# Attention as an 18-unit pipeline in which each engine works on another unit, in a two-layer hybrid transformer step

## The reference

```python
def sink_softmax(logits, sink):
    s = jnp.broadcast_to(sink[None, :, :, None, None], logits.shape[:-1] + (1,))
    p = jax.nn.softmax(jnp.concatenate([s, logits], -1), axis=-1)
    return p[..., 1:]
...
q = axial_rope(q, row, col); k_att = axial_rope(k_att, row, col)     # latent tokens only
...
# latent block i of 128 queries: all 256 cached keys and the blocks i-1, i, i+1 of latent keys
s_c = jnp.einsum('bqkgd,bskd->bkgqs', qblk, ck) * scale
s_w = jnp.where(ok, jnp.einsum('bqkgd,bskd->bkgqs', qblk, kw) * scale, NEG_INF)
p = sink_softmax(jnp.concatenate([s_c, s_w], -1), sink)
out = einsum(p[..., :P], cv) + einsum(p[..., P:], vw)
```

## Time and profile before

| | |
|---|---|
| time, median of 3 runs | 3071.33 us (3064.5 to 3072.36) |
| the profiled execution | time 3057.68 us, span 3055.9 us |
| TensorE | 2703.0 us busy, 88% of the span |
| VectorE | 1314.2 us busy, 43% |
| ScalarE | 1057.0 us busy, 35% |
| GpSimd | 189.6 us busy, 6% |
| mean granted TensorE clock | 0.94 of full speed |

### The profile page before, as it was taken

One profiled execution on the slowest core, in us unless ns is written; L12 is line 12 of the kernel. 1 busy time (PEld: TensorE's weight loads), 2 busy tenths in 40 slices (PEclk: granted clock), 3 DMA queues, 4 the chain that ended last, 5 costly groups with the idle time before them and its releaser, 6 DMA issues.

```text
span 3055.9 us, 72861 instructions
## 1 busy us (share of the span) xinstructions
PE 2703.0 (88%) x32894; PEld 2345.9 (77%) x32894; DVE 1314.2 (43%) x2266; ACT 1057.0 (35%) x1809; POOL 189.6 (6%) x155
## 2 busy tenths in 40 slices
PE   5998699997879999997977899987689999999996
PEld 3985577786679996447955677876589999999995
DVE  2346344443342220004454444533356555555665
ACT  3225334432332120013234434422344444444442
POOL 0001111110000000000000111101010000000010
PEclk8998799997989999998989899988799999999998
DMA  6212033210112221111200131000165555555571
GB/s 243 77 62 113 1 114 113 76 42 2 59 49 76 76 76 62 62 55 59 76 30 1 58 114 59 4 3 4 56 236 209 199 190 207 207 207 186 201 251 74
DMA packets 82717, 304.87 MB, mean 100 GB/s; under 512 B 9376, under 2 KB 9504, under 8 KB 82272
## 3 DMA queue, kind: packets, MB, share of 16 engines
q1 hardware_dynamic: 71072, 257.93, 23.5%
q0 software_dynamic: 11328, 42.21, 3.7%
HBM read 273.10 MB, written 27.00 MB: 98 GB/s over the span
## 4 chain that ended last, share of the span: by engine, by line
PE 84%; DVE 6%; issue 4%; ACT 4%; POOLq 1%; DMA 1%; DVEq 0%; POOL 0%; SPq 0%; PEldq 0%; ACTq 0%
PE ps L401 16%; PE ps L403 16%; PE ps L402 16%; PE ps L1178 6%; PE ps L965 3%; PE ps L978 3%; PE ps L958 3%; PE ps L842 2%; PE ps L641 2%; PE ps L724 1%; PE ps L414 1%; PE ps L781 1%; PE ps L766 1%; PE ps L870 1%; POOLq L2360 1%
## 5 line engine op out<-in xcount | busy, mean ns | idle before, releaser
L1784 DVE TENSOR_TENSOR ring_lo<-ring,w_ffn 128x1024 fp32r<-128x1024 f32 x308 | 374.1, 1224 | 217.2 <-ACT w_ffn L1371 211.3
L401 PE MATMUL ps<-hg_hi,w_ffn 128*128 128x256 f32 x1408 | 401.5, 285 | 0.9 <-DVE hg_lo L2224 0.9
L402 PE MATMUL ps<-hg_lo,w_ffn 128*128 128x256 f32 x1408 | 397.2, 282 | 0.0
L403 PE MATMUL ps<-hg_hi,ring_lo 128*128 128x256 f32 x1408 | 396.7, 282 | 0.0
L1371 ACT ACTIVATE w_ffn<-ring 128x1024 fp32r<-128x1024 f32 x308 | 322.3, 1056 | 198.1 <-PE ps L403 197.3
L401 PEld LDWEIGHTS ps<-hg_hi,w_ffn 128*128 128x128 f32 x1408 | 266.5, 189 | 2.5 <-DVE hg_lo L2224 1.1
L402 PEld LDWEIGHTS ps<-hg_lo,w_ffn 128*128 128x128 f32 x1408 | 265.6, 189 | 1.2
L403 PEld LDWEIGHTS ps<-hg_hi,ring_lo 128*128 128x128 f32 x1408 | 266.2, 189 | 0.0
L401 PE MATMUL ps<-hT_hi,w_proj 128*128 128x320 f32 x672 | 210.9, 314 | 10.0 <-DVE hT_lo L1790 10.0
L401 PE MATMUL ps<-hT_ffn_hi,w_ffn 128*128 128x320 f32 x704 | 214.3, 304 | 5.1 <-DVE hT_lo L1790 5.1
L402 PE MATMUL ps<-hT_lo,w_ffn 128*128 128x320 f32 x704 | 218.6, 310 | 0.0
(11 more groups left out here) (314 smaller groups left out, 5273.2 us busy)
## 6 DMA issues: line engine op xcount, KB each, us to landing
ring<-in_blocks SPq DMA_DIRECT2D x484, 512.0 KB, 3.5
h_rows<-arena POOLq DMA_DIRECT2D x16, 512.0 KB, 10.1
arena<-h_rows POOLq DMA_DIRECT2D x7, 1024.0 KB, 10.2
y_rows<-arena POOLq DMA_DIRECT2D x7, 1024.0 KB, 6.6
x<-in_x_all SPq DMA_DIRECT2D x1, 2560.0 KB, 13.1
h_plain<-arena POOLq DMA_DIRECT2D x1, 2560.0 KB, 11.5
out_y_all<-x POOLq DMA_DIRECT2D x5, 512.0 KB, 2.9
w<-in_low POOLq DMA_DIRECT2D x2, 768.0 KB, 4.9
```

The lines of the kernel that those rows point to most:

```text
L401: nc.tensor.matmul(dst, w_hi, m_hi, start=start, stop=False)
L402: nc.tensor.matmul(dst, w_hi, m_lo, start=False, stop=False)
L403: return nc.tensor.matmul(dst, w_lo, m_hi, start=False, stop=stop)
L1784: V.tensor_tensor(ring_lo[:, n % RING, :], ring[:, n % RING, :], high[:, n % high.shape[1], :], ALU.subtract).then_inc(*E.sig("w_lo"))
```

## The change

There are 18 units instead of 20: the four context units become two, of four heads each. In step t each engine now works on another unit: TensorE does chunk 0 of turning t-3, scores(t), chunk 1 of t-3, the values of t-4, and chunk 2 of t-3. VectorE does the division of t-2, the maxima of t, and the copy out of t-4. ScalarE does the exponentials of t-1 with the copies of the chunks of t-3 between and behind them. A unit's maxima are one instruction instead of two. The copies of the turned cache move from VectorE to ScalarE, after the first exponentials. Of the five rotary parts two come at steps 0 and 1, the others at steps 2, 5 and 9, in PSUM banks 2 and 5 that 512-key units leave free, and the product with the sine is written back to PSUM instead of to a buffer in SBUF. On GpSimd the cosine products are spread likewise around the stores and the clearing transfers.

```diff
+        N_CTXU = 2
+        N_ATT = N_CTXU + 16
+        ROPE_BANK = (2, 5, 2, 5, 5)
+        ROPE_AT = {2: 2, 5: 3, 9: 4}
+        ROPE_BEFORE = {2: 2, 4: 3, 7: 4, 11: 5}
...
             def scores(l, t):
...
                 if t >= 2:
-                    pe.wait_ge(sem["at_exp"], 2 * (n - 1))
-                if t == 4:
-                    pe.wait_ge(sem["rope_ev"], 5 * (l + 1))
+                    pe.wait_ge(sem["at_exp"], n - 1)
+                if t == N_CTXU:
+                    pe.wait_ge(sem["kc_ev"], l + 1)
+                if t in ROPE_BEFORE:
+                    pe.wait_ge(sem["rope_ev"], 5 * l + ROPE_BEFORE[t])
...
             def att_phase(l):
 
+                for t in range(N_CTXU):
+                    scores(l, t)
+                    rope_turn(l, t)
                 pe.wait_ge(sem["misc_in"], 16 * 4 * (l + 1))
...
-                rope_turn(l, 0)
-                rope_turn(l, 1)
-                for t in range(N_PAIRS + 3):
-                    if t < N_PAIRS:
+                for t in range(2, N_ATT + 4):
+                    if 3 <= t < N_ATT + 3:
+                        turn_probs(l, t - 3, 0)
+                    if t < N_ATT:
                         scores(l, t)
-                    if 1 <= t <= 3:
-                        rope_turn(l, t + 1)
-                    if 2 <= t < N_PAIRS + 2:
-                        turn_probs(l, t - 2, 0)
-                        turn_probs(l, t - 2, 1)
-                    if 3 <= t:
-                        attend(l, t - 3)
-                    if 2 <= t < N_PAIRS + 2:
-                        turn_probs(l, t - 2, 2)
+                    if t in ROPE_AT:
+                        rope_turn(l, ROPE_AT[t])
+                    if 3 <= t < N_ATT + 3:
+                        turn_probs(l, t - 3, 1)
+                    if t >= 4:
+                        attend(l, t - 4)
+                    if 3 <= t < N_ATT + 3:
+                        turn_probs(l, t - 3, 2)
...
             def att_phase(l):
-                act.wait_ge(sem["rope_ev"], 5 * l + 2)
...
+                for t in range(N_ATT + 3):
+                    u = t - 1
+                    if 0 <= u < N_ATT:
+                        act.wait_ge(sem["at_max"], l * N_ATT + u + 1)
+                        if u >= 3:
+                            act.wait_ge(sem["at_tr"], chunk_no(l, u - 2))
+                        A(stat(u, 3), stat(u, 1), ACT.Exp).then_inc(*E.sig("act_step"))
+                        for h in range(len(heads_of(u)) - 1):
+                            probs(l, u, h)
+                    probs_ev(l, t - 3, 0)
+                    if 0 <= u < N_ATT:
+                        probs(l, u, len(heads_of(u)) - 1)
+                    probs_ev(l, t - 3, 1)
+                    probs_ev(l, t - 3, 2)
+                    if t == 1:
+                        act.wait_ge(sem["kc_tr"], l + 1)
+                        A(kcT[:, :], ps[:, 6, 0:PAST], ACT.Copy).then_inc(*E.sig("act_step"))
+                        A(kctok[:, :], ps[:, 6, PAST:PAST + P], ACT.Copy).then_inc(*E.sig("act_step"))
+                        A(vtok[:, :, :].rearrange("p i c -> p (i c)"), pair640(3), ACT.Copy).then_inc(*E.sig("kc_ev"))
...
             def rope(l, c):
...
-                V.tensor_tensor(tmp, ps[:, (1, 4)[c % 2], :], C("sin"), ALU.mult).then_inc(*E.sig("dve_step"))
+                V.tensor_tensor(turned, turned, C("sin"), ALU.mult).then_inc(*E.sig("dve_step"))
                 dve.wait_ge(sem["rope_cos"], 5 * l + c + 1)
                 dve.wait_ge(*E.own_last())
-                V.tensor_tensor(dst, dst, tmp, ALU.add).then_inc(*E.sig("rope_ev"))
+                V.tensor_tensor(dst, dst, turned, ALU.add).then_inc(*E.sig("rope_ev"))
...
             def att_phase(l):
...
+                for t in range(N_ATT + 4):
+                    if 2 <= t < N_ATT + 2:
+                        divide(l, t - 2)
+                    if t < N_ATT:
+                        dve.wait_ge(sem["at_s"], l * N_ATT + t + 1)
+                        V.tensor_reduce(by_tile(stat(t, 4)) if t < N_CTXU else stat(t, 4), scores_of(t), AX.X, ALU.max).then_inc(*E.sig("dve_step"))
...
+                    if t < 2:
+                        rope(l, t)
+                    if t in ROPE_AT:
+                        rope(l, ROPE_AT[t])
                     if t >= 4:
...
+                        out_ev(l, t - 4)
```

More of the change, by code:

```diff
@@ L431, in with_flag, with heads_of, query_block, query_tiles @@
                 body()
-        N_PAIRS = 4 * NT
-        def pair_of(t):
-            return (t, -1) if t < 4 else ((t - 4) // 4, (t - 4) % 4)
+        N_CTXU = 2
[3 more added lines that the diff above has]
+        ROPE_BEFORE = {2: 2, 4: 3, 7: 4, 11: 5}
+        def heads_of(t):
+            if t < N_CTXU:
+                return [(2 * t + c, g) for c in range(2) for g in range(2)]
+            return [((t - N_CTXU) // 4, g) for g in range(2)]
+        def query_block(t):
+            return -1 if t < N_CTXU else (t - N_CTXU) % 4
+        def query_tiles(t):
+            c = heads_of(t)
+            return slice(c[0][0], c[-1][0] + 1)
         def own_blocks(blkq):
@@ L741, in scores @@
                 put(0, a0, kcT[rows64(0), :])
-                put(1, a1 + PAST, kT[rows64(1), two[0]])
-                put(0, a0 + PAST, kT[rows64(0), two[0]])
+                put(1, a1 + PAST, kT[rows64(1), two])
+                put(0, a0 + PAST, kT[rows64(0), two])
                 edge = own[0] if blkq > 0 else own[1]
@@ L769, in attend @@
             def attend(l, t):
-                c, blkq = pair_of(t)
-                n = l * N_PAIRS + t
+                first = l * N_ATT
+                heads, blkq = heads_of(t), query_block(t)
                 nk = n_keys(blkq)
@@ L1879, in rope, with divide @@
                 dve.wait_ge(sem["rope_cos"], 5 * l + c + 1)
                 dve.wait_ge(*E.own_last())
-                V.tensor_tensor(dst, dst, tmp, ALU.add).then_inc(*E.sig("rope_ev"))
+                V.tensor_tensor(dst, dst, turned, ALU.add).then_inc(*E.sig("rope_ev"))
+            def divide(l, t):
+                n, nk = len(heads_of(t)), n_keys(query_block(t))
+                dve.wait_ge(sem["at_exp"], l * N_ATT + t + 1)
+                V.tensor_tensor(stat(t, 4), stat(t, 2), stat(t, 3), ALU.add).then_inc(*E.sig("dve_step"))
+                dve.wait_ge(*E.own_last())
+                V.reciprocal(stat(t, 2), stat(t, 4)).then_inc(*E.sig("dve_step"))
+                dve.wait_ge(*E.own_last())
+                if t < N_CTXU:
+                    pr = prob[:, t % 3, 0:n * nk].rearrange("p (h k) -> p h k", h=n)
+                    V.tensor_tensor(pr, pr, stat(t, 2).unsqueeze(2).broadcast_to([P, n, nk]), ALU.mult).then_inc(*E.sig("at_p"))
+                    return
+                for h in range(n):
+                    pr = prob[:, t % 3, h * nk:(h + 1) * nk]
+                    V.tensor_scalar(pr, pr, attst[:, t % 4, 2, h:h + 1], None, ALU.mult).then_inc(*E.sig("at_p" if h == n - 1 else "dve_step"))
@@ L2450, in _ @@
                 next_phase()
-                for c in range(5):
-                    dst = kT[:, CTX:T] if c == 0 else qT[:, c - 1, CTX:T]
-                    pool.wait_ge(sem["rope_mm"], 5 * l + c + 1)
-                    nc.gpsimd.tensor_tensor(dst, dst, C("cos"), ALU.mult).then_inc(sem["rope_cos"], 1)
+                rope_cos(l, 0)
+                rope_cos(l, 1)
                 pool.wait_ge(sem["kc_ev"], l + 1)
```

172 lines of the change are left out of this document (76 added, 96 removed).

## The result

| | before | after |
|---|---|---|
| median | 3069.8 us (3064.5 to 3072.4, 4 runs) | 3013.4 us (3011.1 to 3017.8, 4 runs) |
| profiled execution | 3057.7 us | 3015.1 us |
| TensorE busy | 2703.0 us | 2693.3 us |

The ratio is 0.982, with a 95% interval of 0.9802 to 0.9839: 1.8% faster, where 1.1% had been forecast.

The account below looks back on a forecast made before the run. A VectorE-ScalarE loop was taken as the attention's bound, TensorE next. Start, middle and end gave 97.0 and 92.8 us against 112.5 and 111.5, 34.2 less: 3023.5 from the profile, scaled to 3037 on the median; range 3022 to 3054.

Parts of the forecast that it names:

- The bound: Middle part of attention: a VectorE-ScalarE loop bounds a unit at 5.03 us before; TensorE is the bound after.
- the step: Latent units in the middle part: 18.5 us for four, 4.62 us a unit, at full clock.
- the start: From the attention phase's start to the first latent scores: 6.8 us against 20.9, 14.1 less.
- the last one of the sum: Whole program: the ratio of 3023.5 to the profiled 3057.7 us, applied to the median 3071.3, gives 3037.
- the price of the clock in layer 0: Middle part, layer 0: four steps with TensorE at the low clock level cost 7.7 us more.
- nothing else in the program changes: Outside the attention phases: all engines meet at the phase's end, so what it loses the program loses.
- the loop between VectorE and ScalarE: Middle part before: VectorE's next division waits for ScalarE's exponentials, mean 5.03 us a unit; dividing unit t-2 removes it.
- the 0.1 a unit for hand-offs: Latent steps: added for hand-offs the sum of pieces leaves out, taking four units from 18.1 to 18.5 us.
- The wait behind the short chunk: TensorE's latent steps: chunk 0 follows the short chunk in the same bank, costing 0.63 us twice in four steps.
- the 1.0 us for this: Start: allowance for one rotary sum on VectorE held while GpSimd multiplies, taking 5.8 to 6.8 us.
- The end: From the last unit's scores to the phase's end: 15.5 us against 13.5, 2.0 more, the pipeline being one unit deeper.
- rival 2: Attention phases: the low clock ends early and the 7.7 + 3.5 us are not paid; 3026 us, chance 0.10.

Follow-up runs that it names:

- e2: The kernel before with only the new order in the steps, keeping its 20 units, old start and two reductions; 3054.7 us, ratio 0.9957.
- e3: The changed kernel with the first block of a 640-key unit's scores computed between the short chunk and the next chunk 0; 3008.9 us, ratio 0.981 to before.
- e2b: The changed kernel once more, unchanged, for a second profile and more times; 3014.7 us, ratio 0.9822 to the kernel before.
- e0: The kernel before once more, unchanged, for a second profile; 3067.2 us in its profiled execution.
- f0: The kernel before, unchanged, profiled a third time; attention 239.0 us and recurrent mixer 796.6 us, both layers added.
- e5: The kernel before with twelve dummy transposes on TensorE in each layer's start; 3063.9 us, ratio 0.9993.
- e6: The kernel before with the two reductions of a latent unit joined in one instruction; 3064.0 us, ratio 0.999.
- e1: The kernel before with only the new start, the steps keeping their old order; 3033.6 us, ratio 0.9889.
- f1: The changed kernel with 43 small copies added to VectorE per layer, in the attention's last three steps; 3011.3 us, ratio 0.9847 to the kernel before.

## Why the forecast was right in kind and wrong in size

The bound, the step and the start came out as forecast. The steps that failed are the last one of the sum, which scaled the saving onto the median (13.5 us too high), the price of the clock in layer 0 (some 6 us too high), and "nothing else in the program changes".

**What bounds the kernel: right.** e2 alone removes the loop between VectorE and ScalarE and brings the step from 5.03 to 4.59 us. e3 shows the new bound: take 1.15 us from TensorE's four steps, and the four steps are 1.15 us shorter.

**The step: right.** 4.62 us at full clock was forecast, 4.56 is measured. The sum from rows had given 18.1 us for four units, the trace 18.25, so the 0.1 a unit for hand-offs was too much. The wait behind the short chunk is there, 1.00 us as in the tail of before.

**The start: right, in part by luck.** 6.66 and 6.67 us against 6.8. It is made otherwise than I added it up: no rotary sum was held, so the 1.0 us for this wasn't due, but the first sum waits 0.63 us for its cosine product (216.38), and small hand-offs make up the rest. None of these sums began while a cosine product ran, so whether the new sum would escape isn't shown. What meets GpSimd's product instead is a small operation, as here at the next rotary part in layer 0:

```profile
234.80 1.28 POOL L2420 TENSOR_TENSOR arena<-arena,con 128x512 f32<-128x512 f32 x1
234.92 1.19 DVE L1959 TENSOR_SCALAR small<-small 128x2 f32<-128x2 f32 x1
```

1.19 us where its like takes 0.17, and it ends with the product. That agrees with the Trainium skill, in the page SBUF — State Buffer, section "SBUF: two separate sides": an exclusive lock between a GpSimd instruction and VectorE operations with two SBUF inputs or in a mode that takes both ports.

**The end: 0.9 us too short** in each layer. From the last scores on, the steps took 2.9, 4.2, 4.2, 3.7 and 1.4 us, where I had 2.8, 3.9, 4.1, 3.1 and 1.6. The second has a wait of 0.92 for ScalarE (292.91) where I had 0.78, and the fourth one for VectorE that I had not put in, though the tail of before has it too (325.63): the last values wait until the ones before are copied out.

```profile
303.38 0.66 PE L814 MATMUL ps<-arena,cv 128*64 128x128 f32 x8 [0.48 <-DVE arena L1945]
```

The 13.5 us that I compared with were a misreading: the copy at 325.19 isn't the last. With 15.1 the end costs 1.3 us more than before, and the same forecast of the phases would have given 35.8 us saved instead of 34.2.

**The price of the clock: the term that was mis-sized inside the phase.** "7.7 us in layer 0" was read off one execution of before, in which the low level lasted for some 20 us under full load, with the clearing transfers beside it. In layer 0 of the changed kernel it is gone after 3.4 us, with the transfers running just the same, and the middle part takes 68.6 us, 6.1 less than forecast. In layer 1 it lasts longer (10.2 us) and the part takes 71.1 us against 70.5. Where no clock is lost, in layer 0 of e2b, it takes 67.5 us, against my 67.0 at full clock. So rival 2 held in layer 0, and the transfers, which I named as a possible cause, can fill their share at the full clock. From the start of the phase to its last copy, the time at the low level was 17 to 31 us a layer in the six executions with the old start (before, e0, f0, e2, e5, e6) and 0 to 10 us in the seven with the new one. e2 alone has 27 and 24, e1 alone 7 and 3: it is the new start, not the order, that took most of the low clock away, which I had not put into the sum.

**A piece left out: the phase behind.** "Nothing else in the program changes" was wrong by 5.2 us in the two profiled executions: the stretch behind the last copy is 2.5 and 2.8 us shorter, as the clock falls 4 us behind the last copy instead of 1.4. Most of this is chance of these two executions. Over all of them the stretch takes 7.5 to 10.3 us with the old start (mean 9.6) and 7.5 to 10.4 with the new one (mean 8.9); f0, the kernel before, has 7.5 in layer 0, and e3, with the new start, 10.4. So the change itself accounts for some 1.4 us of it at most, and that isn't shown either.

**The base: the largest part of the miss.** The profile to profile sum is 3057.7 less 34.2, 3023.5 forecast, and 3015.1 measured. Then I scaled by the ratio onto the median, which put 13.5 us on top, as if the changed kernel would lie above its own profile as the kernel before does. It doesn't: its median is 1.7 us under its profiled execution. The miss of 23.6 us is made of 13.5 (base), 8.4 from profile to profile, and 1.7. The 8.4 are 5.5 in the phases (34.2 forecast, 39.7 measured, 1.6 of it from the misread last copy) and 5.2 behind them, less some 2.4 that came back in the rest, most of it in the recurrent mixer.

Why the kernel before lies above its profile is shown in part. Its recurrent mixer took 790.6 us in the execution that I read, and 800.5 and 796.6 in the two others. Over all profiled executions it takes 790.6 to 806.4 with the old start (six, mean 798.8) and 786.0 to 794.7 with the new one (seven, mean 791.0). Two things differ in the trace. The first is the clock: the recurrent mixers spent 94 us at the low level in the execution that I read, and 104 and 107 in the two others. It doesn't separate the old start from the new one, with means of 105 and 107. The second is how long TensorE stands still without a wait. The chain of waits of the kernel before, in the recurrent mixer of layer 1:

```profile
1742.08 0.35 PE ps L899 x24
1742.43 1.14 issue
1743.57 0.46 PE ps L899 x16
1744.03 0.58 PE ps L906 x40
1744.61 1.04 PE ps L842 x71
1745.66 1.55 issue
```

In the middle of like matmuls TensorE stops for over a us and waits for nothing that the trace shows. Such stops of over 0.9 us number 28 to 32 in both recurrent mixers together in the six executions with the old start, and 17 to 24 in the seven with the new one. All stops of this kind over 0.25 us add up to 50.8 us in the mean of the first and 44.2 in that of the second, 6.6 less, where the recurrent mixers differ by 7.8. So most of this difference is in the stops. It is one between groups of kernels, though: for the two kernels alone, three executions of before and two of after, the recurrent mixers differ by 2.3 us. How the start of the attention can change the stops stays open: it isn't the count of TensorE's instructions alone (e5), nor the count of VectorE's in either direction (e6, f1).

## What to carry to other kernels

When two engines wait for each other inside one step, put another unit between them, and price the new step as the sum of the pieces of the engine that is late next, from start-to-start distances; this sum held to 1%. Count pairs of pieces that share one buffer back to back: each pays the full trip through the other engine, and a piece from elsewhere between them removes it. Where a phase comes twice, compare its marks in both: an end part of 13.5 us beside one of 15.1 was a misread row. A sum made on one profiled execution needs that execution's own place among its repeats, phase by phase; scaling a saving by a ratio onto a median adds a guess that is as large as the other terms.

## What was not expected of the hardware

How long TensorE's clock stays low under full load isn't a property of the kernel. In the changed kernel, 4.00 of 4.00 us busy at 1548 to 1552 stood at 0.50, and 2.86 of 4.00 at 236 to 240 at 1.00; in two executions of this one kernel the low level took 3.4 and 0 us of the attention in layer 0, and 10.2 and 3.4 in layer 1. TensorE's stops of over 0.9 us without a wait in dense runs of small matmuls, up to 2.8 us long, come 8 to 17 times in a layer's recurrent mixer, and between the kernels with the old start and with the new one their number differs by a third.
